# RWKV, convolution and attention hybrid on one core: the first stage's four projections as three f32r products, with the lerps split and rewritten in place

## What is computed

```python
def rwkv7_time_mix(h, v_first, mu, w_in, ...):
    xx = token_shift(h) - h
    lerp = lambda j: h + xx * mu[j]
    xr, xw, xk, xv, xa, xg = (lerp(j) for j in range(N_LERP))
    r = xr @ w_in[0]
    k = xk @ w_in[1]
    v = xv @ w_in[2]
    g = xg @ w_in[3]
    ...
    y = wkv7_scan(rh, heads(decay), kh, vh, kk, kk * ah)   # 32 heads of 64, a recurrence over the tokens
    ...
    return y @ w_out, v_first
```

## Time and profile before

| | us |
|---|---|
| median of 3 runs (4590.91 to 4593.27) | 4591.2 |
| the profiled execution | 4586.48 |
| its span | 4584.8 |

### The profile page before, as it was taken

How to read it: one execution, slowest core, us unless ns; L and a number is a source line. 1 busy time by engine, 2 the same in 40 slices (tenths; PEclk the granted TensorE clock), 3 DMA queues, 4 the chain that set the end, 5 groups by cost and what they waited for, 6 DMA issues and landing times. The chain is left out here.

```text
span 4584.8 us, 131580 instructions
## 1 busy us (share of the span) xinstructions
PE 4219.0 (92%) x58346; PEld 3217.2 (70%) x58346; DVE 2370.4 (52%) x5302; ACT 1315.9 (29%) x3044; POOL 274.1 (6%) x308
## 2 busy tenths in 40 slices
PE   7999999999999999998988999999969977877579
PEld 5888888888888888886777887888746643444344
DVE  4556555565555655554215543444255533688842
ACT  2233323332323223222213332232113312433221
POOL 1000000000000000000000000000000000111100
PEclk9999999999999999998999999999989988566789
DMA  2322222222222222221413333333211110000010
GB/s 74 92 68 79 63 88 68 83 64 78 77 79 68 79 68 77 70 79 50 127 37 110 96 96 83 101 96 96 55 42 28 23 37 9 1 1 0 0 46 37
DMA packets 520412, 289.54 MB, mean 63 GB/s; under 512 B 30256, under 2 KB 509728, under 8 KB 519904
## 3 DMA queue, kind: packets, MB, share of 16 engines
q1 hardware_dynamic: 519904, 281.88, 21.3%
HBM read 267.55 MB, written 12.58 MB: 61 GB/s over the span
## 5 line engine op out<-in xcount | busy, mean ns | idle before, releaser
L344 PE MATMUL a_bank<-a_lerps,a_wt 128*128 128x256 f32 x4096 | 1036.9, 393 | 2.4 <-DVE a_lerps L815 2.4
L344 PEld LDWEIGHTS a_bank<-a_lerps,a_wt 128*128 128x128 f32 x4096 | 731.0, 189 | 126.9 <-issue 21.2
L1208 PE MATMUL b_bank<-b_hR,b_wR 128*128 128x512 f32 x1024 | 399.8, 390 | 15.5 <-DVE b_wL L1213 15.5
L1208 PE MATMUL b_bank<-b_hL,b_wR 128*128 128x512 f32 x1024 | 399.7, 390 | 0.0
L1208 PE MATMUL b_bank<-b_hR,b_wL 128*128 128x512 f32 x1024 | 399.5, 390 | 0.0
L931 DVE TENSOR_TENSOR a_iv_X<-a_bank,a_iv_X 128x256 f32<-128x256 f32 x256 | 108.7, 425 | 413.3 <-PE a_bank L448 413.3
L1213 DVE TENSOR_TENSOR b_wL<-b_w,b_wR 128x1024 fp32r<-128x1024 f32 (+1 forms) x144 | 192.4, 1340 | 116.8 <-ACT b_wR L1296 104.0
L692 ACT ACTIVATE a_iv<-a_bank 128x512 f32<-128x512 f32 x192 | 114.7, 597 | 419.1 <-PE a_bank L454 266.2
L1208 PEld LDWEIGHTS b_bank<-b_hR,b_wR 128*128 128x128 f32 x1024 | 193.0, 188 | 56.0 <-issue 16.1
L1208 PEld LDWEIGHTS b_bank<-b_hL,b_wR 128*128 128x128 f32 x1024 | 192.9, 188 | 40.4
L1208 PEld LDWEIGHTS b_bank<-b_hR,b_wL 128*128 128x128 f32 x1024 | 193.0, 189 | 40.2
(11 more groups left out here) (441 smaller groups left out, 8156.7 us busy)
## 6 DMA issues: line engine op xcount, KB each, us to landing
a_wt<-in_a_w_in SPq DMA_DIRECT2D x256, 512.0 KB, 4.2
b_w<-in_b_w_in SPq DMA_DIRECT2D x128, 512.0 KB, 4.0
b_w<-in_b_w_out SPq DMA_DIRECT2D x16, 1024.0 KB, 5.6
rwkv_out<-a_ybuf SPq DMA_DIRECT2D x64, 128.0 KB, 5.7
m_w<-in_a_w_out SPq DMA_DIRECT2D x16, 512.0 KB, 4.0
s_wp<-in_w_in SPq DMA_DIRECT2D x12, 512.0 KB, 3.8
a_xtok<-in_x SPq DMA_DIRECT2D x4, 1024.0 KB, 7.1
m_two<-rwkv_out SPq DMA_DIRECT2D x16, 256.0 KB, 3.0
```

What stands on the lines that cost most here:

```text
L344: r = mm(o, wt[:, j, c, :], src[:, c, :], start=(c == 0), stop=(c == ND - 1))
L1208: m = nc.tensor.matmul(o, a, b, start=(first and i == 0), stop=(last and i == 2))
```

## The change

1. **Projections in three f32r products.** Weights and lerps are each kept as a rounded part (R, f32r) and a low part (L, the difference, f32r). `project` does R·R, R·L and L·R for each chunk in place of one f32 matmul. 32x3 = 96 matmuls of 128x256 a step in place of 64 records.
2. **Weights.** ScalarE rounds each `wt` (128x1024) to `wR` (`round_weights`, after the P1/P2 copy for k, r, g and after the value copy for v), GpSimd subtracts (`low_weights`, after the root and, for v, after the bonus). SyncE reloads `wt` when its low part is done, a step earlier than before; the low-rank weights come behind the first of them; stores move from m - 3 to m - 4, `load_x` from step 3 to 4.
3. **Lerps in place.** The second `lerps` buffer is gone. Each lerp is written by VectorE to one of three `tmp` buffers (two chunks at a time), rounded by ScalarE (`round_lerp`) and subtracted by GpSimd (`low_lerp`), 16 units a pass. k, r and the first of g are rewritten in step 14 and at its end, the rest of g and v in step 15, just behind the last reader of the old pass. The shifts all stand in step 13, and `xx` lives in `xtok`.
4. **The first unit** does the same one after the other, in the order k, r, g, v.

```diff
-        lerps = sb("lerps", [P, 2, 4, ND, PASS])
-        lerp = [{n: lerps[:, b, i, :, :] for i, n in enumerate("rkvg")} for b in range(2)]
-        wt = sb("wt", [P, 4, ND, P])
+        lerpR, lerpL = ({n: sb(f"lerp{x}_{n}", [P, ND, PASS], F32R) for n in "krgv"} for x in "RL")
+        wR, wL = ({n: sb(f"w{x}_{n}", [P, ND, P], F32R) for n in "krgv"} for x in "RL")
+        tmp = [sb(f"tmp{i}", [P, 2, PASS]) for i in range(3)]
+        wt = {n: sb(f"wt_{n}", [P, ND, P]) for n in "krgv"}
...
-        xx = [sb(f"xx{i}", [P, PASS]) for i in range(2)]
+        xx = xtok[:, :, :].rearrange("p a b -> p (a b)").rearrange("p (c n) -> p c n", n=PASS)
...
-                    sp.wait_ge(s["prk"], m + 1)
-                    sp.dma_start(lwa2[w_rows, :], d["a_w2"][0][:, cols]).then_inc(s["wk"], 16)
...
+                    for i, name in enumerate(LERPS):
+                        if m:
+                            sp.wait_ge(s["wL"], (m - 1) * len(LERPS) + i + 1)
+                        sp.dma_start(wt[name][:, :, :], w_in[W_IN[name]][:, :, cols]).then_inc(s["w" + name], 16)
+                        if i == 0:
+                            if m:
+                                sp.wait_ge(s["pwa"], m)
+                            sp.dma_start(lwa2[w_rows, :], d["a_w2"][0][:, cols]).then_inc(s["low"], 16)
+                            sp.dma_start(lwa2[a_rows, :], d["a_a2"][0][:, cols]).then_inc(s["low"], 16)
+                    if m >= 4:
+                        store(m - 4)
...
-                def project(o, j, src, lo, hi):
+                def project(o, m, name, lo, hi):
+
+                    if lo == 0:
+                        pe.wait_ge(s["wL"], m * len(LERPS) + LERPS.index(name) + 1)
+                    if m % NF == 0:
+                        pe.wait_ge(s["lo"], unit(m // NF, name, (hi + 1) // 2 - 1) + 1)
                     for c in range(lo, hi):
-                        r = mm(o, wt[:, j, c, :], src[:, c, :], start=(c == 0), stop=(c == ND - 1))
+                        mm(o, wR[name][:, c, :], lerpR[name][:, c, :], start=(c == 0), stop=False)
+                        mm(o, wR[name][:, c, :], lerpL[name][:, c, :], start=False, stop=False)
+                        r = mm(o, wL[name][:, c, :], lerpR[name][:, c, :], start=False, stop=(c == ND - 1))
                     return r
...
+                def round_weights(m, names=LERPS):
+                    for name in names:
+                        act.wait_ge(s["w" + name], 16 * (m + 1))
+                        sem, count = free(name, 0)
+                        act.wait_ge(s[sem], count + m)
+                        a(wR[name][:, :, :], wt[name][:, :, :], ACT.Copy).then_inc(s["wR"], 1)
+
+                def round_lerp(ps, name, i):
+                    n = unit(ps, name, i)
+                    act.wait_ge(s["tmp"], n + 1)
+                    sem, count = free(name, ps)
+                    act.wait_ge(s[sem], count)
+                    a(lerpR[name][:, 2 * i:2 * i + 2, :], tmp[n % 3][:, :, :], ACT.Copy).then_inc(s["hi"], 1)
...
                     if m is not None:
                         rates(m, e)
+                    lerps(15, ("r", 2), ("r", 3), ("g", 0))
...
                         decays(m, e)
+                    lerps(15, ("g", 1), ("g", 2), ("g", 3))
...
                         gate(m, e)
+                    lerps(14, ("k", 0), ("k", 1), ("k", 2))
+                    lerps(15, ("v", 0), ("v", 1), ("v", 2), ("v", 3))
                     act.wait_ge(s["pP12"], ready)
                     copy_two(pr12, 4, "P12", scale=-1.0)
-                    prep, at = prepared(n)
+                    lerps(14, ("k", 3), ("r", 0), ("r", 1))
...
                     if m is not None:
+                        if m + 1 < STEPS:
+                            round_weights(m + 1, "krg")
                         vals(m, e)
+                        if m + 1 < STEPS:
+                            round_weights(m + 1, "v")
...
+                def low_weights(m, names=LERPS):
+                    for name in names:
+                        pool.wait_ge(s["wR"], m * len(LERPS) + LERPS.index(name) + 1)
+                        low(wL[name][:, :, :], wt[name][:, :, :], wR[name][:, :, :]).then_inc(s["wL"], 1)
...
-                    if prep and 10 <= at <= 13:
-                        shift(prep, 2 * (at - 10))
-                        shift(prep, 2 * (at - 10) + 1)
+                    if prep and at == 14:
+                        for name, i in (("k", 0), ("k", 1), ("k", 2), ("k", 3), ("r", 0), ("r", 1)):
+                            low_lerp(prep, name, i)
+                    if prep and at == 15:
+                        for name, i in (("r", 2), ("r", 3), ("g", 0), ("g", 1), ("g", 2), ("g", 3)):
+                            low_lerp(prep, name, i)
+                        for i in range(ND // 2):
+                            low_lerp(prep, "v", i)
                     if m is not None:
+                        if m + 1 < STEPS:
+                            low_weights(m + 1, "krg")
                         bonus(m, pair[1 - par])
+                        if m + 1 < STEPS:
+                            low_weights(m + 1, "v")
+                        if prep and at == 13:
+                            for c in range(ND):
+                                shift(prep, c)
...
+                def lerped(ps, *units):
+                    for name, i in units:
+                        n = unit(ps, name, i)
+                        v.wait_ge(s["xx"], ps * ND + 2 * i + 2)
+                        if n >= 3:
+                            v.wait_ge(s["lo"], n - 2)
```

More of the change, by code:

```diff
@@ L413, in first @@
                         turn_x(0, i, 2 + i)
[L414 removed]
                     low_in(0, 0, ND, 6)
[L416 to L417 removed]
+                    for c in range(0, ND, 2):
+                        keys(m, c, c + 2)
                     low_rank(m)
[L419 to L422 removed]
+                    for c in range(0, ND, 2):
+                        receptance(m, c, c + 2)
+                    for c in range(0, ND, 2):
+                        gate(m, c, c + 2)
+                    for c in range(0, ND, 2):
+                        vals(m, c, c + 2)
                     key_norm(m)
@@ L746, in _, with low @@
             def _(pool):
+                def low(l, x, rounded):
+                    return nc.gpsimd.tensor_tensor(l, x, rounded.bitcast(F32), ALU.subtract)
                 def bonus(m, e):
```

115 lines of the change are left out of this document (64 added, 51 removed).

## The result

The changed kernel takes 4762.7 us (median; 4755.5 to 4769.2), the kernel before 4591.1 (4588.6 to 4593.3): a ratio of 1.037, 95% interval 1.036 to 1.039, slower by 172 us. The sign was forecast, the size was not: the time lies 28 us above the range.

What follows compares the result with a forecast made beforehand. The prediction took TensorE's streaming to bound the stage. Fills -174, recurring wait +149, lerps +32 and +42, first unit +12 gave +61 us on 4591.2: 4652, rounded to 4650, range 4555 to 4735.

Steps and rivals of the forecast that it cites:

- Part 1: Projections: f32r matmuls of 256 columns at 0.117 us each save 2.72 us a step, 174 us in 64 steps.
- Parts 3 and 4: Plain steps: GpSimd's subtractions delay the root and hold X1 by the port; TensorE waits 2.4 us, 149 us in 62 steps.
- the sum: Whole kernel: all terms added, -174 + 149 + 32 + 42 + 12 = +61 us.
- rival (a): Plain steps: GpSimd subtractions under about 1.8 us each bring no regular wait; about 4475 us, chance 0.25.
- If X1 takes 0.42 us, part 4 is: Sign in a plain step: X1 should last over 2 us; at 0.42 us the port's hold would be wrong.
- the zero of the layout: A step's first mask, from which the layout counted: values' subtraction ends at 4.10, root 5.21, S2/E2 copy 8.03 us.
- rival (c): Pass seams: long waits drop TensorE's clock to 1.2 GHz, 20 us more a pass; about 4750 us, chance 0.07.
- Part 5: Lerps: steps 8 to 13 +32 us, steps 14 and 15 with the seam +42 (24 to 72), first unit +12 (8 to 16).
- Part 2: ScalarE's four roundings, 4.2 us a step, are covered; earlier weight loads and later stores cost nothing.

Runs made afterwards that it cites:

- e1: Changed kernel with GpSimd's low part of v's weights moved behind the root and VectorE's diagonal: 4646.6 us, ratio 1.012.
- e2: As e1, but v's low part does not wait for VectorE's diagonal: 4720.4 us, ratio 1.030.
- e13: e5 with the first unit's weight subtractions on VectorE and pass-change work laid elsewhere, lerps r2, r3 and g0 in step 15: 4517.4 us, ratio 0.985.
- e5: e1 with r's load freed from the wait for the rates' product, g's and v's held until the inverse's last turn: 4560.6 us, ratio 0.994.
- e12: Changed kernel with the loads alone changed as in e5, v's low part still ahead of the root: 4727.5 us, ratio 1.030.
- e7: Kernel before with three extra 512 KB loads a step, read by nobody, beside the inverse's 32-row blocks: 4646.0 us, ratio 1.013.
- e11: Kernel before with eleven idle ScalarE copies ahead of the S2/E2 copy in every step but the last: 4714.5 us, ratio 1.028.
- e8: Kernel before with eight idle ScalarE copies ahead of the S2/E2 copy in every step but the last: 4656.7 us, ratio 1.014.

## Why the prediction was right in sign and wrong in size

**Part 1** was right in kind: 0.120 us a matmul, the upper of the bounds from the earlier trace rows, not 0.117. A step without gaps is 2.4 us shorter, not 2.72. That is 149 us instead of 174: 25 us of the miss.

**Parts 3 and 4** named the mechanism, its place and its order: the root, X1 held to the end of v's subtraction, the diagonal, the columns, the copy, 31.98 us for such a step. The wait is 1.98 us against 2.44 by the sum, 25 us the other way in 62 steps. The GpSimd row holds (2.38 for the 2.36 of the earlier trace rows), so rival (a) was out by its own condition; e1 and e2 show queue and hold. Two details were off. "If X1 takes 0.42 us, part 4 is" wrong was too narrow a sign: in most steps X1 takes 0.41 and the hold sits on the variance just ahead of it (2.40 us for 0.15), with the same end. And the hold already catches the state's copy at the end of the step, 1.17 us instead of 0.19, which moves the first mask, the zero of the layout: counted from it v's subtraction ends at 3.04 instead of 4.10, the root at 4.20 instead of 5.21 and the S2/E2 copy at 6.82 instead of 8.03, while TensorE wants it at 4.89 instead of 5.59. The wait came out near because both of its ends moved the same way.

**The clock is the step that failed.** The sum counted an idle microsecond as a microsecond and left the 1.2 GHz level to rival (c), with a chance of 0.07, and there only behind the pass changes. The row that I took as speaking against it has 0.99, not the 1.00 that I wrote, with the 17 us at 1.2 GHz at the stage's very end; above all it came from a stage in which TensorE hardly waited, and said nothing of one with a wait of 2 us in each step. The lower clock followed in 30 of the 37 plain steps and cost 97 us in all (94 by the steps that differ in nothing else). The whole is then, in the terms of the trace: -149 for the fills, 124 for 62 waits of 2.0 us, 67 for all other idle time, 97 for the clock, 31 for the first unit and 6 behind the stage, +176. Of the 115 us between this and the +61 of the sum, the clock is 97, the first unit 19; the rest cancels (fills +25, wait -25, part 5 within the steps -7, behind the stage +6). Rival (c) gave the nearest time, 4750, but by luck: it had the lower clock behind the pass changes alone, and the pass changes at their upper ends.

**Part 5.** Against the plain steps of the same kernel, and beyond what they cost before, steps 8 to 13 took 1.03 us more each, 19 us for 32, and steps 14 and 15 took 7.9 more each, 48 for 42 (a share of the clock's price is in both), inside the bounds (24 to 72); e13 shows that a good part was order, not work: by the same measure steps 14 and 15 took 9.1 us more each in e5 and 5.8 in e13, steps 8 to 13 0.8 and 0.2. (A reading in that part was off by little: the earlier trace rows has 0.47 us for a turned copy, not 0.42.) The first unit cost 30.7 us for 12 and lies outside 8 to 16. Of the 34 us of GpSimd's work that I had added up, 29 came behind the shifts; they took 42, from 39.6 to 81.8 us, because the turns (1.02 each) and a wait of 5.84 for the first rounding of r, which ScalarE does behind the rates and decays, stand between, and a subtraction beside VectorE's lerps takes 2.5 to 2.8 us instead of 2.36. Bounds on the parts of such a chain bound nothing as long as its turns are left out.

**Part 2** was right that the roundings and the loads hold nothing up themselves. But "I cost both at nothing" asked only whether the data came in time, not what else uses the DMA engines then. The loads moved onto the densest stretch of instructions: 35 us here (e12), and 86 once the rest is mended (e5).

**What is left open.** The 97 us are a remainder over all steps, backed by the 19 steps that can be compared directly. What decides whether a wait of 2 us lets the clock fall (its length to a tenth of a us, when it comes, or the kind of fills around it) was not settled. That the gaps come and go with bulk data beside the dense stretch is shown by moving the data both ways; how the hardware shares the DMA engines between data and instruction packets is not.

## What to carry to other kernels

Where one engine runs without a gap, price a new regular wait by its length and by what the clock does after it, since the clock added 97 us to 191 us of idle time here. An operation in the free time of VectorE that works from SBUF to SBUF is free only if GpSimd is idle then; put the long GpSimd operation behind the last VectorE result that somebody waits for. When an edit moves loads, look for what TensorE issues in that stretch: gaps on "issue" in the middle of a group may be instructions that came late; holding two loads back in each step was worth 86 us in e5, against the 149 of the faster matmuls.

## What the runs showed of the hardware

- The instruction queue brings packets of 16 KB, half of them 220 to 290 of TensorE's matmuls and weight loads apart. Beside a burst of 1 to 1.5 MB at 320 to 350 GB/s (e1, e7) TensorE stood still for 0.8 to 2.8 us in its densest stretches and mostly went on 1.2 to 1.6 us after such a packet had landed.
- An f32r matmul of 128x256 with its own weight load starts every 0.120 us, and 0.213 at the 1.2 GHz level, so the clock doesn't quite double it.
- The granted clock fell to 1.2 GHz in 33 of 41 steps of the changed kernel with a wait of 1.96 to 2.06 us, in 7 of 62 of the kernel before with a wait of 1.81 to 1.94 us (e11), and in none of 62 with 1.0 us (e8). A step with one such stretch is 1.4 us longer. The Trainium skill ("TensorE: Matmul & The Clock Gate", section "Part 1: The HAM clock gate") lists 1.2 GHz as what an idle TensorE gets; these runs show it behind waits that were short against the step.
- VectorE's X1, a tensor_tensor with two inputs in SBUF, takes 0.41 us alone and up to 2.60 beside a GpSimd subtraction of 128x1024; a tensor_scalar with one input in SBUF is held too: the S_all copy of 128x64 took 1.17 instead of 0.19, the variance of 128x4 2.40 instead of 0.15. The Trainium skill's rule of the shared port ("SBUF — State Buffer", section "Who interferes with whom"), weighed in the prediction, agrees for the operations with two inputs. For the two tensor_scalars it would ask for a two-port mode, and no trace here shows the mode.
